# Attention bias left unscaled and its mask set by memsets; modulation sums taken one at a time between weight units

## The reference

```python
mod = jax.nn.silu(c) @ w_ada[l] + b_ada[l]                      # 6 * 1024 values
sh1, sc1, gt1, sh2, sc2, gt2 = jnp.split(mod, 6, axis=-1)
h = modulate(rmsnorm(x, norm1_g[l]), sh1, sc1)                  # h * (1 + scale) + shift
proj = h @ w_in[l]                                              # ka, qa, va, qkb, vb, gates ...
...
s = jnp.einsum("blhd,bkhd->bhlk", qj, kj) * scale + bias        # scale = 64 ** -0.5
valid = (j * CHUNK + k_idx - pad) >= 0                          # chunks of 64 tokens
...
x = x + gt1 * (y @ w_out[l])
h2 = modulate(rmsnorm(x, norm2_g[l]), sh2, sc2)
x = x + gt2 * peer_ffn(h2, ...)                                 # begins with h2 @ w_peer_q
```

## Time and profile before

| | |
|---|---|
| median of 3 runs | 2571.97 us (2568.14 to 2577.08) |
| profiled execution, its own time | 2572.46 us |
| its span | 2570.6 us |
| TensorE busy | 2289.4 us, 89% |
| VectorE busy | 1745.9 us, 68% |
| ScalarE busy | 1294.2 us, 50% |
| GpSimd busy | 253.2 us, 10% |

### The profile page before, as it was taken

The page is one execution under the profiler, slowest core; times in us unless marked ns, Lnnn a source line. Parts: engine busy times, 40 slices in busy tenths (PEclk is TensorE's granted clock), DMA queues, the critical chain, the costliest instruction groups (busy, mean ns, idle before and its releaser), DMA issues.

```text
span 2570.6 us, 47820 instructions
## 1 busy us (share of the span) xinstructions
PE 2289.4 (89%) x15056; PEld 2078.7 (81%) x15056; DVE 1745.9 (68%) x3636; ACT 1294.2 (50%) x2846; POOL 253.2 (10%) x286
## 2 busy tenths in 40 slices
PE   3887689999997699999889978799999986899998
PEld 3785579999997578888778936799999975788887
DVE  7665553888886966666643446638888869766665
ACT  3345244555455755555534554344554557555554
POOL 2000000000004910000010000000000029300000
PEclk7998789999999999999989979899999999999999
DMA  8761134555552045555334502345555530355554
GB/s 314 255 236 57 46 127 146 180 180 184 180 184 80 0 160 191 195 191 193 131 106 157 180 0 69 120 147 179 180 181 187 179 115 0 106 191 192 194 191 153
DMA packets 106071, 389.60 MB, mean 152 GB/s; under 512 B 12032, under 2 KB 12160, under 8 KB 105232
## 3 DMA queue, kind: packets, MB, share of 16 engines
q1 hardware_dynamic: 104688, 381.73, 43.5%
q10 hardware_dynamic: 992, 4.88, 0.5%
q0 software_dynamic: 320, 2.13, 0.2%
HBM read 387.64 MB, written 1.05 MB: 151 GB/s over the span
## 4 chain that ended last, share of the span: by engine, by line
PE 80%; POOL 8%; DVE 6%; ACT 3%; DMA 1%; issue 1%; SPq 0%; ACTq 0%; POOLq 0%; DVEq 0%
PE ps L539 18%; PE ps L506 16%; PE ps L501 16%; PE ps L503 16%; PE ps L543 9%; POOL scores L405 8%; DVE big L1131 1%; PE ps L618 1%; PE ps L598 1%; DMA big<-ada_in 1%; DVE act_lo L1184 1%; DVE lo L1108 1%; PE ps L608 1%; PE ps L646 1%; PE ps L495 1%
## 5 line engine op out<-in xcount | busy, mean ns | idle before, releaser
L841 ACT ACTIVATE hi<-raw 128x512 fp32r<-128x512 f32 x1356 | 776.3, 621 | 94.5 <-PE ps L506 87.0
L1108 DVE TENSOR_TENSOR lo<-raw,hi 128x512 fp32r<-128x512 f32 x844 | 553.3, 697 | 192.0 <-ACT hi L841 190.9
L501 PE MATMUL ps<-act_hi,hi 128*128 128x256 f32 x3376 | 557.7, 289 | 84.1 <-DVE act_lo L1184 43.4
L506 PE MATMUL ps<-act_hi,lo 128*128 128x256 f32 x3376 | 554.4, 287 | 27.9 <-DVE lo L1108 27.9
L503 PE MATMUL ps<-act_lo,hi 128*128 128x256 f32 x3376 | 553.0, 287 | 0.0
L501 PEld LDWEIGHTS ps<-act_hi,hi 128*128 128x128 f32 x3376 | 478.2, 197 | 90.7 <-DVE act_lo L1184 69.0
L506 PEld LDWEIGHTS ps<-act_hi,lo 128*128 128x128 f32 x3376 | 475.4, 196 | 30.8 <-DVE lo L1108 30.6
L503 PEld LDWEIGHTS ps<-act_lo,hi 128*128 128x128 f32 x3376 | 476.7, 196 | 0.0
L866 ACT ACTIVATE big<-ps 128x256 f32 (+1 forms) x354 | 136.2, 385 | 589.3 <-PE ps L506 589.3
L1378 DVE TENSOR_TENSOR lo<-raw,hi 128x512 fp32r<-128x512 f32 x512 | 329.1, 688 | 135.4 <-ACT hi L841 129.2
L539 PE MATMUL ps<-hi,act_hi 128*128 128x512 f32 x1024 | 398.7, 389 | 0.0
(11 more groups left out here) (180 smaller groups left out, 1371.8 us busy)
## 6 DMA issues: line engine op xcount, KB each, us to landing
raw<-u SPq DMA_DIRECT2D x256, 512.0 KB, 3.3
raw<-v SPq DMA_DIRECT2D x256, 512.0 KB, 3.4
raw<-front SPq DMA_DIRECT2D x166, 512.0 KB, 3.3
big<-ada_in SPq DMA_DIRECT2D x48, 512.0 KB, 5.5
big<-biasA_in ACTq DMA_DIRECT2D x1, 2048.0 KB, 11.1
xT<-xT_in ACTq DMA_DIRECT2D x1, 1024.0 KB, 9.7
big<-keys_in ACTq DMA_DIRECT2D x1, 1024.0 KB, 14.4
scores<-memT_in POOLq DMA_DIRECT2D x1, 1024.0 KB, 5.3
```

Of the source, the lines that this page charges most:

```text
L501: pe.matmul(out_ap, hi_l(k), hi_r(k), start=(first and k == 0), stop=False, skip_group_check=True)
L506: mm = pe.matmul(out_ap, lo_l(k), hi_r(k), start=False, stop=(last and k == n - 1), skip_group_check=True)
L841: act.activation(hi[:, s, :, :], raw[:, rs, 4 * h:4 * h + 4, :], ACT.Copy).then_inc(hi_done, 1)
L1108: dve.tensor_tensor(lo[:, s, :, :], raw[:, rs, 4 * h:4 * h + 4, :], hi[:, s, :, :].bitcast(F32), ALU.subtract).then_inc(lo_done, 1)
```

## The change

- **Bias.** The multiplication by 8 on GpSimd is gone. The query half of the ka_qa results is multiplied by 1/8 when ScalarE takes it out of PSUM, and VectorE's L1211 has the factor -1 in place of -1/8. ScalarE's two groups of ka_qa are both written out (`peel=2`).
- **Mask.** The four selects become three memsets of rectangles, 64 partitions by 8x192, 8x128 and 8x64 elements. The fourth, which had nothing to mask, is left out.
- **Modulation.** Tiles 16 to 47 are no longer done in bursts of four but one at a time, each behind the two halves of one unit: after units 0, 1, 2, 4, 5, 6 of ka_qa and qkb, 0, 1, 2 of va and vb, 0, 1, 2, 6, 10, 14 of gates1 (24 tiles), and after every second unit of pq1 (the last 8, which had been done by the end of gates1's second group). SP issues each tile's load right behind the load of the same unit. The small addition still comes once in 4 tiles. On VectorE and SP these runs are written out in full.

```diff
-ADA_IN_RUN = {"ka_qa": (16, 2), "va": (24, 1), "qkb": (28, 2), "vb": (36, 1), "gates1": (40, 2)}
+def place_ada():
+
+    at, tile = {}, ADA_FIRST
+    for name, units in (("ka_qa", (0, 1, 2, 4, 5, 6)), ("va", (0, 1, 2)), ("qkb", (0, 1, 2, 4, 5, 6)),
+                        ("vb", (0, 1, 2)), ("gates1", (0, 1, 2, 6, 10, 14)), ("pq1", range(0, 16, 2))):
+        for u in units:
+            at[name, u] = tile
+            tile += 1
...
@@ SP
-            def load_ada(g, first):
-
-                for j in range(ADA_RING):
-                    if not (is_static(g) and g * ADA_RING + first < ADA_RING):
-                        sp.wait_ge(ada_used, g * ADA_RING + (first + j - ADA_RING + 1))
...
+            def load_ada(tile):
+
+                if tile >= ADA_RING:
+                    sp.wait_ge(ada_used, tile - ADA_RING + 1)
+                sp.dma_start(ada_raw[tile % ADA_RING], ada_in[tile:tile + 1].rearrange("a p k -> (a p) k"))\
+                    .then_inc(ada_loaded[tile % ADA_RING], 16)
...
                         sp.dma_start(raw[:, s, :, :], source(r, u)).then_inc(raw_in[s], 16)
-
-                    if r.name in ADA_IN_RUN:
-                        first, n = ADA_IN_RUN[r.name]
-                        if is_static(g) and g < n or r.units // GROUP == n:
-                            load_ada(g, first)
-
-                groups(sp, r, body, peel=2 if r.name == "gates1" else 1)
+                        if r.name in ADA_RUNS and (r.name, u) in ADA_AT:
+                            load_ada(ADA_AT[r.name, u])
+
+                groups(sp, r, body, peel=r.units // GROUP if r.name in ADA_RUNS else 1)
@@ GpSimd
-            link(pool.tensor_scalar(biasA, biasA, 8.0, None, ALU.mult))
             for qt in range(QT):
                 for half in range(2):
                     limit = CHUNK * (2 * qt + half + 1)
-                    v = biasA[64 * half:64 * half + 64, :, qt, :]
-                    link(select(v, [[0, 8], [-1, T]], limit - 1, 0, NEG))
+                    if limit < T:
+                        link(pool.memset(biasA[64 * half:64 * half + 64, :, qt, limit:T], NEG))
@@ item("a", h)
-                            scale=64 ** -0.5, v=lambda kt: va[:, kt, 64 * h:64 * h + 64], dh=64,
+                            scale=1.0, v=lambda kt: va[:, kt, 64 * h:64 * h + 64], dh=64,
@@ ScalarE
-            run("ka_qa", to(kaqa))
+            run("ka_qa", lambda u, p: act.activation(kaqa[:, u, :], p, ACT.Copy, scale=1.0 if u < 4 else 64 ** -0.5),
+                peel=2)
@@ VectorE
-            def ada(g, first):
-
-                for j in range(ADA_RING):
...
+            def ada(tile):
+
+                j = tile % ADA_RING
+                dve.wait_ge(ada_loaded[j], 16 * (tile // ADA_RING + 1))
+                dve.tensor_tensor_reduce(out=ada_raw[j], in0=ada_raw[j], in1=c_row, scale=1.0, scalar=0.0,
+                                         op0=ALU.mult, op1=ALU.add, accum_out=ada_sum[:, j:j + 1])\
+                    .then_inc(ada_used, 1)
+                if j < ADA_RING - 1:
+                    return
+                dve.wait_ge(ada_used, tile + 1)
+                dve.tensor_tensor(mod[:, tile - j:tile + 1], ada_sum[:, :],
+                                  cols[:, COLS["b_ada"][0] + tile - j:COLS["b_ada"][0] + tile + 1], ALU.add)\
+                    .then_inc(mod_s, 1)
...
-                    if name in ADA_IN_RUN:
-                        first, n = ADA_IN_RUN[name]
-                        if is_static(g) and g < n or r.units // GROUP == n:
-                            ada(g, first)
+                        if name in ADA_RUNS and (name, g * GROUP + j) in ADA_AT:
+                            ada(ADA_AT[name, g * GROUP + j])
```

More of the change, by code:

```diff
@@ L71 @@
 ADA_FIRST = 16
-ADA_IN_RUN = {"ka_qa": (16, 2), "va": (24, 1), "qkb": (28, 2), "vb": (36, 1), "gates1": (40, 2)}
+def place_ada():
[5 more added lines that the diff above has]
+            tile += 1
+    assert tile == 48
+    return at
+ADA_AT = place_ada()
+ADA_RUNS = ("ka_qa", "va", "qkb", "vb", "gates1", "pq1")
 def place_runs():
@@ L333, in free @@
                 sp.wait_ge(lo_done, (n - RAW + 1) * 2)
-            def load_ada(g, first):
-                for j in range(ADA_RING):
-                    if not (is_static(g) and g * ADA_RING + first < ADA_RING):
-                        sp.wait_ge(ada_used, g * ADA_RING + (first + j - ADA_RING + 1))
-                    sp.dma_start(ada_raw[j], ada_in[bass.ds(g * ADA_RING + (first + j), 1)]
-                                 .rearrange("a p k -> (a p) k")).then_inc(ada_loaded[j], 16)
+            def load_ada(tile):
[3 more added lines that the diff above has]
+                    .then_inc(ada_loaded[tile % ADA_RING], 16)
             def source(r, u):
@@ L351, in source @@
                 return w[bass.ds(u + r.row0, 1)].rearrange("a p k c -> (a p) k c")
-            for g in range(ADA_FIRST // ADA_RING):
-                load_ada(g, 0)
+            for tile in range(ADA_FIRST):
+                load_ada(tile)
             for r in RUN_LIST:
@@ L841, in weight_hi, with run @@
                 act.activation(hi[:, s, :, :], raw[:, rs, 4 * h:4 * h + 4, :], ACT.Copy).then_inc(hi_done, 1)
-            def run(name, evict=None):
+            def run(name, evict=None, peel=1):
                 r = RUNS[name]
@@ L860, in run @@
                 else:
-                    groups(act, r, body)
+                    groups(act, r, body, peel=peel)
                 if evict:
@@ L1125, in convolution @@
                         dve.wait_ge(conv_s, tap + 1)
-            def ada(g, first):
-                for j in range(ADA_RING):
[L1130 to L1139, removed]
+            def ada(tile):
[10 more added lines that the diff above has]
+                    .then_inc(mod_s, 1)
+                dve.wait_ge(mod_s, tile // ADA_RING + 1)
             def run(name, evict=None):
@@ L1168, in run @@
                 else:
-                    groups(dve, r, body, peel=5 if name == "gates1" else 1)
+                    groups(dve, r, body, peel=r.units // GROUP if name in ADA_RUNS else 1)
                 if evict:
@@ L1385, in _ @@
             dve.wait_ge(silu_s, 1)
-            for g in range(ADA_FIRST // ADA_RING):
-                ada(g, 0)
+            for tile in range(ADA_FIRST):
+                ada(tile)
             def gains(k, name):
```

## The result

The changed kernel took 2541.48 us (median of 4 runs, 2536.99 to 2543.26) against 2570.93 for the kernel before (4 runs): 29.4 us less, a ratio of 0.9883 with a 95% interval of 0.9867 to 0.9899. In a second set of runs it was 2543.21 (4 runs) against 2569.07 (9 runs), 25.9 less, 0.9897 (0.9882 to 0.9912). The forecast was 2546, 26.6 less, with a range of 2541 to 2554. The direction and the size came out, since 26.6 lies between the gains of the two sets, but the times lie at the very low end of the range; the profiled execution, 2540.84, is just outside it.

What follows compares the result with a forecast made beforehand. The prediction took TensorE, with 80% of the chain, to pace nearly all stages. Removing 18.3 us in ka_qa and 8.3 of other bursts, all else 0, gave 2572.5 - 26.6 = 2545.9, predicted as 2546, range 2541 to 2554.

Steps and rivals of the forecast that it cites:

- GpSimd's work and the burst in ka_qa: In ka_qa, GpSimd's bias work holding VectorE, with a burst of sums, costs TensorE 18.3 us including slow groups; all removed.
- My own ground for 0: Memsets in ka_qa, 2.7 us, cost 0 even if they hold VectorE, being shorter than the 3.25 us tap that costs nothing.
- The other bursts: Three later TensorE waits, at 117.59, 160.61 and 176.31 us, from four sums in a row: 1.35 + 1.3 + 5.7 = 8.3 removed.
- pq1: Eight sums moved into pq1 cost 0 us, each 1.23 fitting VectorE's 1.58 us wait per unit; 9.8 if uncovered.
- SP's order: Early unit loads wait for sums of tiles 12 to 14, unit 3's issued by 33 us; no cost taken.
- the four episodes: TensorE's delays in ka_qa (18.3 us) and at 117.59, 160.61 and 176.31 us (8.3 together), 26.6 in all.
- the 0 to 1.3 us: Before the first norm, fewer loads in flight may gain 0 to 1.3 us; 0 was taken.
- 1.3 us gained at the start, and a little clock: The ground for the likeliest case's lower bound of 2544 us, against the forecast of 2546.
- DMA as the holder: Rival: DMA traffic of bias and keys, not GpSimd, stops VectorE near 49 us, so the stop stays; 2562.9 us, 3%.
- starving: Rival: single tile loads ahead of weight units each delay TensorE by 1.2 us, 38.4 in all; 2584 us, 3%.
- the second case: A part comes back: late units 5 to 7 (3.6) with slow clock (1.7), or half of pq1's sums (4.9); 2551 on, 13%.

Runs made afterwards that it cites:

- e1: The kernel before with the bias half alone: no GpSimd multiplication, three memsets, queries scaled at eviction, sums still in bursts of four; 2552.41 us against 2569.07.
- e3: The changed kernel with each of the three memsets done eight times in a row; 2543.57 us against the changed kernel's 2543.21.
- e5: The changed kernel with one GpSimd multiplication of the whole bias by 1.0 put back ahead of the memsets; 2551.51 us.
- e2: The changed kernel with the multiplication by 8, four selects and old scales put back, so only the sums are new; 2555.14 us.
- early tiles: The changed kernel with the first 16 modulation tiles loaded into 16 buffers of their own; 2538.05 us.

## Why the prediction was right, and where not

*What bounds.* TensorE paces the kernel and a wait removed early is gained at the end: the 27.55 us at the end of gates1 arrived whole, and stood at 27.68 around 1300 us.

*GpSimd's work and the burst in ka_qa, 18.3 us.* The mechanism is shown by e1 (17 forecast, 16.7 measured), e3 and e5: instructions of GpSimd that read the bias hold VectorE for nearly their whole length (a pair of halves takes 9.6 to 9.9 us beside the multiplication), memsets don't (1.29 beside 24 us of them). The term was right in size but is not a sum of two costs: the bias half alone takes away all but the 1.5 us of a burst without GpSimd beside it, and with the sums taken singly the same GpSimd work costs 11.0 in place of 18.3. My expectation of e2 came from leaving this out. The rule of the Trainium skill that I weighed ("SBUF — State Buffer", Who interferes with whom) holds: VectorE's instructions with two inputs in SBUF are held by GpSimd's reads and not by its writes. My own ground for 0, the margin that hides a 3.25 us tap, wasn't needed; the three memsets took 2.96 us, not 2.7.

*The other bursts, 8.3 us.* All three waits are gone, and TensorE waits for no `lo` before the end of gates1. By the same matmuls in both profiles the four episodes are shorter by 18.3, 1.4, 1.4 and 5.6 us: 26.7, where the sum said 26.6.

*pq1, 0.* The eight sums there cost nothing. TensorE's waits for `lo` in pq1 are 0.4 us in one case, as before; a pair of halves that follows a sum still waits for ScalarE:

```profile
351.59 1.29 DVE L1117 TENSOR_TENSOR lo<-raw,hi 128x512 fp32r<-128x512 f32 x2 [0.44 <-ACT hi L849]
```

VectorE has 0.44 us to spare there and was 1.22 poorer, as the sum of 1.23 and a gap of 1.58 had said.

*SP's order, 0.* Units 1 to 3 were issued at 28.31, 30.04 and about 31.7, a little earlier than the 33 I had allowed, and ScalarE waited for no weight. The first matmul came 0.40 us earlier (40.39 against 40.79); in the other profiles with this order of loads it came at 39.91 to 40.54, so some of the 0 to 1.3 us was there.

*What failed is the low end of the range: the allowance for what lies outside the four episodes.* The sum put the whole stretch behind gates1 at nothing, and the low end rested on "1.3 us gained at the start, and a little clock". In the profiled pair the gain beyond the sum was 31.7 - 26.6 = 5.1 us. Before the transposes it has two parts of clock, of opposite sign. At the start of gates1 a wait of 2.51 us stands in both kernels; before, slow groups followed 1.6 us behind it:

```profile
145.32 0.71 PE L501 MATMUL ps<-act_hi,hi 128*128 128x256 f32 x4 [2.51 <-ACT hi L841]
...
146.90 1.05 PE L501 MATMUL ps<-act_hi,hi 128*128 128x256 f32 x4
147.75 1.05 PE L503 MATMUL ps<-act_lo,hi 128*128 128x256 f32 x4
148.61 1.05 PE L506 MATMUL ps<-act_hi,lo 128*128 128x256 f32 x4
```

In the first profile of the changed kernel the groups behind the same wait are all at the upper level:

```profile
126.26 0.71 PE L509 MATMUL ps<-act_hi,hi 128*128 128x256 f32 x4 [2.51 <-ACT hi L849]
...
127.77 0.64 PE L509 MATMUL ps<-act_hi,hi 128*128 128x256 f32 x4
```

Three groups at 0.85 us from start to start in place of 0.48 are 1.1 us, with the part-slow ones beside them about 1.5. Against it, the first matmuls stayed slow for three groups longer than before (the last slow group starts at 45.65 in place of 43.49), 1.1 us. Together with the 0.40 that makes 26.6 + 1.5 - 1.1 + 0.4 = 27.4, against 27.55 measured. Neither clock part is shown to be the change's: in the second profile of the changed kernel the groups behind the 2.51 us wait are slow as before, and the first matmuls are fast by 42.8 us, sooner than before. That the sum and the place of the transposes agree so well is in part luck.

The third part is the stretch behind gates1: 4.15 us in one pair of profiles, 1.9 in the other. That is the term that put the profiled execution below the range. It arises behind some 1300 us, where the diff changes no instruction, and two executions of one program differ by 2.3 us behind gates1. What decides when the clock falls and rises in a given execution stays open. With 1.5 us for gates1 and 4 for the stretch behind it beside the 1.3 at the start, a low end near 2539 would have been the honest one (an estimate from these profiles).

*The rivals.* DMA as the holder is out by e1. No weight was waited for, so starving didn't happen, and nothing of the second case ("a part comes back") was seen.

## What to carry to other kernels

Look at what GpSimd does beside VectorE: here an instruction of GpSimd that read the bias stopped VectorE's instructions with two inputs for nearly its whole length, a memset not at all, so move scaling to where the data is evicted anyway and build masks by writing. Work for a feeding engine is free as long as each piece fits into the gap behind one unit; the same work in bursts is not, and what stands in the queue behind a hold decides how much of it is felt. Two edits that shorten the same episode don't add; and price the slow clock behind every wait that may come or go, not only the waits. Give the range room for the clock in stretches that you don't touch.

## What the runs showed of the hardware

- Behind the same wait of 2.51 us of TensorE groups at the lower level of the clock followed in five profiles (kernel before, sums half alone, eight times the memsets, changed kernel again, one multiplication) and not in three (bias half alone, changed kernel, early tiles). They cost 1.3 to 1.5 us. Two profiles of one program also differ by 2.3 us behind gates1. A difference of one or two us between single profiles of this kernel says nothing.
- Beside one GpSimd multiplication of 128x4096 elements a pair of `lo` halves took 9.63 to 9.93 us. One half of the pair bears it all (9.03, 9.13 and 9.32 us); the other takes its usual 0.7. The held half ended 1.2 us before GpSimd's recorded end in all three profiles. Where a first half had started together with the multiplication, the multiplication took 11.12 us in place of 10.57.
- Four selects with four VectorE instructions between them took 9.28 us for GpSimd and 9.48 for VectorE: the two engines took turns, one instruction each. Beside sums in place of halves the four selects took 10.85.
